# One stacked-block kernel on Trainium2: the first up projection's norm and its first two chunks reordered, last squares kept apart, GpSimd's weight passes in two halves

## What is computed

```python
def rms_norm(x, w):
    xf = x.astype(jnp.float32)
    y = xf * lax.rsqrt(jnp.mean(xf * xf, axis=-1, keepdims=True) + EPS)
    return y.astype(x.dtype) * w

def modulate(x, norm_w, shift, scale):
    return rms_norm(x, norm_w) * (1 + scale) + shift

def conv_ffn(h, w_up, conv_w, conv_b, w_down):
    up = h @ w_up
    gate, val = up[..., :D_FF], up[..., D_FF:]
    ...
    return (jax.nn.silu(gate_c) * val) @ w_down
```

## Time and profile before

| | |
|---|---|
| median of 3 runs | 2578.45 us (2570.19, 2578.45, 2580.16) |
| the profiled execution | 2579.7 us, its span 2577.9 us |
| granted TensorE clock, mean | 0.956 of full |
| PE busy | 2451.1 us, 95% |
| DVE busy | 1023.3 us, 40% |
| ACT busy | 894.9 us, 35% |
| POOL busy | 864.7 us, 34% (527 instructions) |
| chain that ended last | PE 85%, DVE 6%, ACT 3%, DMA 2%, POOL 2%, issue 2% |

### The profile page before, as it was taken

The page is one execution under the profiler, slowest core; times in us unless marked ns, Lnnn a source line. Parts: engine busy times, 40 slices in busy tenths (PEclk is TensorE's granted clock), DMA queues, the critical chain, the costliest instruction groups (busy, mean ns, idle before and its releaser), DMA issues.

```text
span 2577.9 us, 36722 instructions
## 1 busy us (share of the span) xinstructions
PE 2451.1 (95%) x14405; PEld 2035.1 (79%) x14405; DVE 1023.3 (40%) x1669; ACT 894.9 (35%) x1387; POOL 864.7 (34%) x527
## 2 busy tenths in 40 slices
PE   6999999987999999999999999999999999999997
PEld 3876976976888888888887778888887886688766
DVE  4762673144233223334223236322345004752173
ACT  5433343233222222324411344222344225633462
POOL 2453364223222222323231214444444441134302
PEclk9999999998999999999877899999999999999999
DMA  7177168111212211212210002233332321122211
GB/s 279 59 267 271 50 245 327 62 49 41 61 61 65 65 58 64 65 58 70 75 34 1 1 17 82 90 98 94 94 98 74 127 97 62 51 66 82 72 49 66
DMA packets 56952, 234.92 MB, mean 91 GB/s; under 512 B 6336, under 2 KB 7616, under 8 KB 56064
## 3 DMA queue, kind: packets, MB, share of 16 engines
q1 hardware_dynamic: 56592, 232.44, 26.7%
q0 software_dynamic: 240, 0.79, 0.1%
HBM read 231.11 MB, written 2.10 MB: 90 GB/s over the span
## 4 chain that ended last, share of the span: by engine, by line
PE 85%; DVE 6%; ACT 3%; DMA 2%; POOL 2%; issue 2%; SPq 0%; DVEq 0%; ACTq 0%; POOLq 0%
PE ps L849 16%; PE ps L850 15%; PE ps L851 15%; PE ps L1477 4%; PE ps L1479 4%; PE ps L1480 4%; PE ps L1298 2%; PE ps L602 2%; PE ps L1371 2%; DMA XB<-ada_dram 2%; PE ps L1673 1%; PE ps L1660 1%; PE ps L1597 1%; PE ps L886 1%; PE ps L887 1%
## 5 line engine op out<-in xcount | busy, mean ns | idle before, releaser
L460 POOL TENSOR_TENSOR w_low<-ring,w_high 128x1024 fp32r<-128x1024 f32 (+2 forms) x267 | 625.5, 2344 | 1308.9 <-ACT w_high L453 1308.9
L453 ACT ACTIVATE w_high<-ring 128x1024 fp32r<-128x1024 f32 (+2 forms) x267 | 274.6, 1032 | 987.7 <-PE ps L851 653.0
L849 PE MATMUL ps<-h_high,w_high 128*128 128x512 f32 x1040 | 411.5, 396 | 12.7 <-DVE h_low L705 9.0
L850 PE MATMUL ps<-h_low,w_high 128*128 128x512 f32 x1040 | 408.6, 393 | 0.0
L851 PE MATMUL ps<-h_high,w_low 128*128 128x512 f32 x1040 | 407.7, 392 | 0.0
L849 PEld LDWEIGHTS ps<-h_high,w_high 128*128 128x128 f32 x1040 | 197.4, 190 | 60.1 <-DVE h_low L705 9.9
L851 PEld LDWEIGHTS ps<-h_high,w_low 128*128 128x128 f32 x1040 | 197.3, 190 | 42.0
L850 PEld LDWEIGHTS ps<-h_low,w_high 128*128 128x128 f32 x1040 | 197.6, 190 | 38.4
L1477 PE MATMUL ps<-hidden,w_high 128*128 128x512 f32 (+1 forms) x504 | 178.6, 354 | 0.0
L1479 PE MATMUL ps<-hidden,w_high 128*128 128x512 f32 (+1 forms) x504 | 178.5, 354 | 0.0
L1480 PE MATMUL ps<-hidden,w_low 128*128 128x512 f32 (+1 forms) x504 | 178.3, 354 | 0.0
(11 more groups left out here) (443 smaller groups left out, 5144.6 us busy)
## 6 DMA issues: line engine op xcount, KB each, us to landing
XB<-ada_dram SPq DMA_DIRECT2D x84, 768.0 KB, 6.0
ring<-up_dram SPq DMA_DIRECT2D x88, 512.0 KB, 3.6
ring<-down_dram SPq DMA_DIRECT2D x44, 512.0 KB, 3.6
ring<-winE_dram SPq DMA_DIRECT2D x32, 512.0 KB, 3.3
ring<-win_dram SPq DMA_DIRECT2D x20, 512.0 KB, 3.6
ring<-winC_dram SPq DMA_DIRECT2D x20, 512.0 KB, 3.3
arena<-ada_dram SPq DMA_DIRECT2D x12, 768.0 KB, 21.1
XB<-xl_dram SPq DMA_DIRECT2D x2, 2048.0 KB, 9.5
```

The lines of the kernel that those rows point to most:

```text
L453: nc.scalar.activation(WH[p][:, 0:L], RAW[p][:, 0:L], ACT.Copy).then_inc(w_hi, 1)
L460: nc.gpsimd.tensor_tensor(WL[p][:, 0:L], RAW[p][:, 0:L], WH[p][:, 0:L].bitcast(F32), ALU.subtract)\
L849: nc.tensor.matmul(bank[:, 0:n], wh[:, cols], hi, start=(k == 0), stop=False)
L850: nc.tensor.matmul(bank[:, 0:n], wh[:, cols], lo, start=False, stop=False)
```

## The change

Four things, in five functions. In n1, n3, n5 and n6 (LAST_APART) the last tile's squares are no longer added to SA: TensorE multiplies SA (tiles 0 to 6) and then the last tile's squares by the ones. For that `out_squares` squares the last tile before it splits the next stage's second chunk. In n1 both roots are inverted before anything is scaled. In up0 the first round is written out: chunks 0 and 1 over the latents, then both over the context, then chunks 2 and 3 over both; the loop does the other 10 rounds. And `split_lo` makes two instructions of half the columns each, in every stage.

```diff
--- before.py
+++ after.py
@@ -146,6 +146,7 @@
 NORM_STAGES = [x for x in SUMS if x in ("n0", "ro0", "ro1", "n1", "n2", "nlat", "nqk", "n3", "n4", "nB", "n5", "n6")]
 
 ADDED = ("n0", "n1", "n3", "n5", "n6")
+LAST_APART = ADDED[1:]
 
 PAIRED = (("n2", 0), ("n4", 0))
 
@@ -457,8 +458,10 @@
             p, _ = split_use(stage, k, pairs)
             L = SPLIT[stage][1]
             nc.gpsimd.wait_ge(w_hi, 2 * pairs + (SPLIT_BEFORE[stage] + k + 1))
-            nc.gpsimd.tensor_tensor(WL[p][:, 0:L], RAW[p][:, 0:L], WH[p][:, 0:L].bitcast(F32), ALU.subtract)\
-                .then_inc(raw_spent[p], 1)
+            for at in range(0, L, L // 2):
+                to = slice(at, at + L // 2)
+                ins = nc.gpsimd.tensor_tensor(WL[p][:, to], RAW[p][:, to], WH[p][:, to].bitcast(F32), ALU.subtract)
+            ins.then_inc(raw_spent[p], 1)
 
         def await_parts(eng, stage, k, pairs=0):
             p, used = split_use(stage, k, pairs)
@@ -529,7 +532,8 @@
 
         def last_square(stage, k, j):
 
-            return stage not in ADDED and k == batches(stage)[batch_of(stage, k)][-1] and j == len(ITEMS[stage][k][0]) - 1
+            last = k == batches(stage)[batch_of(stage, k)][-1] and j == len(ITEMS[stage][k][0]) - 1
+            return last and (stage not in ADDED or stage in LAST_APART)
 
         def item_width(stage, k):
             return ITEMS[stage][k][0][0].shape[-1]
@@ -584,12 +588,12 @@
             batch = batches(stage)[b]
             ones = C("ones64")[:, 0:P:64] if g == 2 else C("ones")[:, 0:1]
             at = column_at(stage, k)
-            tiles_ = [KT - 1] if stage in ADDED else range(1, KT, 2) if (stage, k) in PAIRED else range(len(srcs))
+            tiles_ = [KT - 2, KT - 1] if stage in LAST_APART else [KT - 1] if stage in ADDED else range(1, KT, 2) if (stage, k) in PAIRED else range(len(srcs))
             now = tiles_ if some is None else some
             begins = k == batch[0] and now[0] == tiles_[0]
             bank = open_bank(pe, *mean_sum(stage, b)) if begins else bank_ap(*mean_sum(stage, b))
             for j in now:
-                if stage in ADDED:
+                if stage in ADDED and not (stage in LAST_APART and j == KT - 1):
                     await_square_used(pe, square_use(stage, k, j))
                     src = added(stage, k)
                 else:
@@ -713,7 +717,7 @@
 
         def scale_parted(stage, k):
 
-            if stage != "n0":
+            if stage not in ("n0", "n1"):
                 invert(stage, k)
             for j in range(KT + 2):
                 if j == KT - 1 and k == 0 and stage in DEFERRED:
@@ -1446,13 +1450,17 @@
                 ns = len(segs)
                 if norm in DEFERRED:
                     unscaled_two(pe, norm)
-                    for c in range(2, 4):
-                        split_features(pe, up, c, up, ns * c, KT, P, h_parts(norm), segs,
-                                       ready=h_there(pe, norm) if c == 2 else None)
-                with pe.Fori(norm in DEFERRED, FT // 2) as i:
+                else:
+                    for s in segs:
+                        for c in range(2):
+                            split_features(pe, up, c, up, ns * c + s, KT, P, h_parts(norm), (s,),
+                                           ready=h_there(pe, norm) if c == 0 else None)
+                for c in range(2, 4):
+                    split_features(pe, up, c, up, ns * c, KT, P, h_parts(norm), segs,
+                                   ready=h_there(pe, norm) if c == 2 and norm in DEFERRED else None)
+                with pe.Fori(1, FT // 2) as i:
                     for c in range(4):
-                        split_features(pe, up, c, up, ns * c, KT, P, h_parts(norm), segs, loops=i, pairs=2 * i,
-                                       ready=h_there(pe, norm) if c == 0 and norm not in DEFERRED else None)
+                        split_features(pe, up, c, up, ns * c, KT, P, h_parts(norm), segs, loops=i, pairs=2 * i)
 
                 for x in range(2):
 
@@ -1978,12 +1986,15 @@
 
                 load_table(ROOT)
                 for k in range(KT):
-                    split_hi(stage, k + 2) if k + 2 < KT else after and split_hi(after, k + 2 - KT)
+                    if k < KT - 1:
+                        split_hi(stage, k + 2) if k + 2 < KT else after and split_hi(after, k + 2 - KT)
                     for s in range(segs):
                         await_taken(act, stage, segs * k + s)
                         square(norm, s, k)
                     if norm in DEFERRED:
                         u_high(norm, (k,))
+                if after:
+                    split_hi(after, 1)
                 for s in range(segs):
                     root(norm, s)
 
@@ -2558,7 +2569,7 @@
                             taken(STT(X[s][:, k, :], bank[:, 0:n], scalar(k, s), X[s][:, k, :], ALU.mult, ALU.add),
                                   stage, g)
                     for s in segs:
-                        if k >= 2:
+                        if 2 <= k < KT:
                             add_square(norm, s, k - 1)
                     if norm in DEFERRED and k:
                         u_low(norm, (k - 1,))
@@ -2659,6 +2670,8 @@
             dve.wait_ge(x_in, 64)
             add_out("wout0", (0, 1), lambda k, s: mod[:, 0, 16 + k, s:s + 1], "n1")
             for s in range(2):
+                invert("n1", s)
+            for s in range(2):
                 scale_parted("n1", s)
             ffn(0, (0, 1), "n2")
             scale_parted("n2", 0)
```

## The result

The changed kernel takes 2551.83 us (median of 6 runs, 2549.49 to 2557.0); the kernel before, run beside it, 2576.36 (6 runs, 2567.89 to 2580.16). The ratio is 0.9916, 95% interval 0.9892 to 0.9939: the medians differ by 24.5 us, the ratio says about 22, and 8.65 were worked out. That is clear of the noise and under 2%. The profiled execution took 2556.1 us, its span is 2554.3 and its mean granted clock 0.962, against 2579.7, 2577.9 and 0.956 before. PE busy went from 2451.1 to 2440.7 us, DVE from 1023.3 to 980.1, POOL from 864.7 to 931.1.

The account below looks back on a forecast made before the run. TensorE, busy 95% of the span, bounds the kernel; only its gaps and half-clock stretches can be won. 8.75 + 2.0 - 0.5 + 0.2 + 0.9 + 0.9 - 3.6 = 8.65 us, giving 2570.0; range 2566 to 2574, with two rivals 2562 to 2577.

Parts of the forecast that it names:

- Part 1: First up projection: last square not added, root earlier, so latent scaling starts 2.2 us earlier (bounds 0.5 and 3.0).
- part 2: First up projection: both roots and latents first; chunk 2 starts at 635.7 against 644.45, 8.75 us saved with the earlier scaling.
- Part 3: Last square apart in the other stages: 0.5 us lost over n3 and n5, 0.2 won at n6.
- part 4: Weight passes in halves, every stage: 2.0, 0.9 and 0.9 us won from VectorE's lock-outs, 3.6 lost.
- Low part 4: VectorE's low part of tile 4 in n2 to n5: 1.0 us earlier, worth 0.5 each, 2.0 in all.
- The two terms of 0.9: Shorter VectorE lock-outs at the gains of the start and before the second block's first output projection: 0.9 us won each.
- the losses: VectorE stepping in where TensorE waits for a pass: 1.1 us per value round, 0.9 first key chunk, smaller waits; 3.6.
- The third rival: Second down projection: VectorE between halves makes passes late; about 2611 us if handing over costs 0.9 over; chance 0.04.
- 0.06: Cost in us per extra GpSimd instruction estimated from the skill's page, where the profile rows say 0.15.
- the signs that were named as wrong: Latent scaling later than 614, chunk 2 later than 639, or waits for low weights well over 10 us in all.
- The first rival: Up projection worth 9.6 us, four low parts 1.1 each, fewer losses: 14.6 us won, 2563.9; chance 0.20.
- part 4's terms ahead of A: Halved passes early in the kernel: 0.9 us won at the gains of the start, 1.1 lost in each value round.

Follow-up runs that it names:

- e4: The kernel before with only the last square apart and squared ahead of the weight split; 2567.71 us, ratio 0.9975.
- e8: The kernel before with only both roots inverted at once, chunk 0 still taking latents and context in turn; 2571.57 us, ratio 0.9979.
- e13: The kernel before with two spare matmuls (0.43 us) ahead of the work behind which the first attention's 1.40 us gap lies; 2570.02 us, ratio 0.9977.
- e2: The kernel before with only the weight passes in halves; 2557.46 us, ratio 0.9941.
- e5: The kernel before with two useless matmuls filling TensorE's 1.40 us gap ahead of the first attention; 2568.93 us, ratio 0.9975.
- e11: The kernel before with the weight passes in halves and two useless matmuls filling the first attention's gap; 2556.96 us, ratio 0.9941.
- e14: The changed kernel with whole weight passes and two spare matmuls (0.43 us) ahead of the work before the first attention's gap; 2559.33 us, ratio 0.9941.
- e3: The kernel before with both roots inverted at once and the first two chunks latents first, passes whole; 2559.24 us, ratio 0.9952.
- e7: The changed kernel with whole weight passes put back in five stages (win0, win1, wmlp, qb, kvb); 2560.97 us, ratio 0.9945.
- e15: The kernel before with two spare matmuls (0.43 us) right behind the first attention's gap, as a control; 2568.62 us, ratio 0.9979.
- the two filled kernels: The kernel before and the changed kernel, each with two useless matmuls filling the first attention's gap; 2568.93 and 2550.16 us.

## Why the prediction was wrong

**Part 1 and part 2 held.** Sum 8.75, measured 9.0 (38.99 to 29.99). The mean started after 1.27 us (1.21 worked out), at the full level; scaling 2.46 earlier (2.2); the wait for chunk 2's low weights 0.88 (1.1). Taken by themselves, the last square apart brings 3.0 (e4), both roots at once 6.0 (e8) and the new order on top only 0.75.

**Part 3** is small either way. The wait at n6 went from 2.33 to 1.53, which about pays for the longer mean, as said.

**Two steps failed: part 4's size, and the clock that the sum left out.** The sum had no term for the granted clock behind the first up projection. That is the larger miss and comes third below. Part 4's sum was 2.0 + 0.9 + 0.9 - 3.6 = 0.2 us. Between kernels that both lack the attention's fall, the halves alone are worth 13.0 us from A on (e13 less its 0.43, against e2), or 17.7 if e5 is taken for the kernel before; in the medians 12 (e5 and e11). On top of the other parts they are worth 7.7 (e14 less its 0.43, against after). Three things went wrong.

First, the places. Low part 4 was to bring 0.5 in each of four stages; idle there is 2.23 as before in n3, went from 2.39 to 2.24 in n5 and from 2.06 to 2.24 in n4, and only in n2 from 3.18 to 2.23: 0.9 in all, not 2.0. The mechanism was right (VectorE's wait for the pass is halved, 1.92 to 0.83), but GpSimd's odd part is late by the same amount. The real gains are where VectorE's instruction was alone on the path: n1's adds (2.4 us in e2; in the changed kernel, where that last add is gone, the halves cost 0.3 there, 29.68 to 29.99), and the last unscaled tile of n4 (L759, 1.83 to 0.75 us), which I had not looked at. The two terms of 0.9 came as said in TensorE's waits: 5.43 to 4.49 us behind the gains of the start, 2.08 to 1.00 ahead of the second block's output projection.

Second, the losses. They were to be 3.6 us; the waits for a pass, 4.6 us in 6, became, in the waits of the whole span:

```profile
PE ps L853 <- POOL w_low L463: 7.6, 7, 2.3
```

3.0 us more, with n1's 0.88 in it, so 2.1. In the value rounds each round's two waits grew from 0.92 to 1.64 us, and the first key chunk's from 1.69 to 2.28: the mechanism as said, at 0.7 and 0.6 instead of 1.1 and 0.9. The third rival, slower by one wait per chunk of the second down projection, needed a handing over that costs GpSimd more than 0.4 us. VectorE does step in there at nearly every chunk, and the pair takes 3.52 us for it where the pass took 2.40. But 3.52 is two free halves (2.54) and 0.98, no more than VectorE's own 1.1, so the handing over cost nothing beyond it, and those waits did not come. The halving itself costs 0.1 to 0.15 (2.49 to 2.54 us against 2.37 to 2.43). The Trainium skill, GPSIMD Engine Reference, "3.1 Elementwise", from which the prediction estimated 0.06, is below that; this trace's numbers decide.

Third, and largest, the clock, which belongs to no part of the sum. I took the granted clock for unchanged everywhere but in the first up projection. From A on, TensorE spent 135.4 us at half level (mean of before's two) and spends 105.0 now; with halves alone it is 94.4. Half of that difference, 15 us, is the most that it can have given; idle gave 15.1 (67.65 to 52.5); together 30.3, of which 24.5 came out. The other 6 are longer means and work that was not bound by the clock in the first place, as the attention's first stretch: 20.5 us at half level there cost 8.5. It is the largest single piece: 8.5 there and 1.6 at the low record ahead of n3 that goes with it, 10 us, and it lay neither in the sum nor in the range. None of the signs that were named as wrong came either: they watch starts and waits, none the clock. The halves as such aren't the cause of the fall: e3 has none and lacks the fall, e7 has most of them and has it. The rest comes in pieces of 1 to 3 us behind stalls that became shorter; n4 is the largest, 4.0.

So of 24.5 us, by the place where they arise, 9.0 are the first up projection, 10.5 hang on that fall (8.5, 1.6 and 0.4 behind it), and 5 are stalls and clock of the later stages, mostly the halves' work. What the change is worth without the fall is less certain than that split. By places it is 14.0; against after, e13 less its 0.43 gives 14.2, e15 less its 0.43 gives 17.8, e5 18.8, and the two filled kernels 23.0 in A..end and 18.8 in the medians. These versions of the kernel before without the fall differ by 4.7 us among themselves, because short low stretches come and go elsewhere, 1 to 3 us each. The first rival, in favour, has 14.6, the low end of this, and not by its terms; that it came nearest is luck in part. Whether the fall comes hung on less than half a microsecond of matmuls, which I couldn't have read from the kernel before; that it might, and what it would then be worth, could be read from 1411.6 to 1432.0.

**Open.** A itself, before which the change has only its halves, lies between 598.0 and 612.6 in the seventeen profiles, with no order by kernel, so one profile's span alone can't tell 10 us. What part 4's terms ahead of A (0.9 won at the gains, 2.2 lost in the value rounds) made of the time can't be told for the same reason. The two kernels with halves alone have A..end 23 us shorter than before, but medians only 17 lower; for e5 the two agree (5.7 and 6.1). Where the halves' missing 6 go, before A or in executions that were not kept as a trace, wasn't measured.

## What to carry to other kernels

Sum a forecast twice: once over idle, and once over the time at the lower clock level behind each idle, because a stall of 1.4 us can cost 8.5 more behind it and a shortened one gives part of that back. Look for clock falls far from the edit: where a short gap is followed by a long low stretch, any shift of the work ahead may remove or bring it, so put its price in the range, and close such a gap with spare matmuls, in several ways, before two versions are compared: the three versions of this kernel before without its fall spread over 4.7 us. In this kernel splitting a long GpSimd instruction paid where a VectorE instruction alone on TensorE's path waited behind it, and gave nothing where GpSimd's own next result was wanted right after.

## What the runs showed of the hardware

- One gap of 1.40 to 1.44 us in dense work was followed by 20.5 us at 0.50 of the clock in five profiles and by none in eight, at the same place of the same work (three of the eight with 0.43 us added beside it); with the gap filled down to 0.12 to 0.14 us it stayed away in four of four.
- The clock stayed up when work was added: 0.43 us of matmuls, ahead of the gap (e13, e14) or behind it (e15), one profile each.
- A waiting VectorE instruction is let in between two GpSimd ones, and GpSimd's pair is longer for it: 2.98 or 3.52 us instead of 2.49 to 2.54 for two halves. A copy of four columns took 0.72 us behind a half; the next one, of two columns and with no GpSimd instruction to wait for, took 0.17. The Trainium skill, SBUF — State Buffer, "SBUF: two separate sides", says that whichever engine starts first holds the shared port pair for its whole instruction; this trace agrees (1.83 us behind the whole pass, 0.75 between halves).
- From the end of the output projection on, two executions agree within 0.2 to 0.9 us in 1950 to 1970, while the 600 us ahead of it spread over 14.5 across the seventeen profiles.
